# Norms summed between the weight tiles and handed on in blocks of four chunks, in a two-block transformer kernel

## The reference

```python
def rms_norm(x, g):                       # _rmsnorm of the second block is the same
    return x * lax.rsqrt(jnp.mean(x * x, axis=-1, keepdims=True) + 1e-6) * g

# first block: dilated attention and pooling, then 128*128 experts
xn = rms_norm(h, norm1_g) * (1 + scale1) + shift1        # norm a1
...
h = h + gate1 * (merged @ w_out)
xn2 = rms_norm(h, norm2_g) * (1 + scale2) + shift2       # norm b1
h = h + gate2 * peer_ffn(xn2, ...)                       # peer_wq, top-k, gelu(x @ down.T) * gates @ up
x = rms_norm(h, final_g)                                 # norm f1
# second block: joint attention with 256 context tokens, then a gated convolution FFN
hx = _rmsnorm(x, norm1_w) * (1 + s1) + sh1               # norm a2
hc = _rmsnorm(ctx, norm1_w) * (1 + s1c) + sh1c           # norm ctx
...
x = x + g1 * (heads @ w_o)
h2 = _rmsnorm(x, norm2_w) * (1 + s2) + sh2               # norm b2
x = x + g2 * (silu(conv3(h2 @ w_up_gate)) * (h2 @ w_up)) @ w_down
return _rmsnorm(x, final_w)                              # norm f2
```

## Time and profile before

| | |
|---|---|
| three runs | 4014.66, 4017.24, 4024.36 us; median 4017.24 us |
| the profiled execution | 4012.41 us, of which the span on the engines is 4010.6 us |
| TensorE matmul busy | 3630.9 us of the span |
| VectorE, ScalarE busy | 2671.8 us, 1656.7 us |
| mean granted TensorE clock | 0.961 of full speed |

### The profile page before, as it was taken

One profiled execution on the slowest core, in us unless ns is written; L12 is line 12 of the kernel. 1 busy time (PEld: TensorE's weight loads), 2 busy tenths in 40 slices (PEclk: granted clock), 3 DMA queues, 4 the chain that ended last, 5 costly groups with the idle time before them and its releaser, 6 DMA issues.

```text
span 4010.6 us, 73869 instructions
## 1 busy us (share of the span) xinstructions
PE 3630.9 (91%) x27694; PEld 3473.7 (87%) x27694; DVE 2671.8 (67%) x4416; ACT 1656.7 (41%) x2865; POOL 174.6 (4%) x240
## 2 busy tenths in 40 slices
PE   0899999883699999999999999889978989999998
PEld 0898888882599999999999999878945989999998
DVE  7875434589887878777777878652247566666554
ACT  0542112431254444444444544442226455555443
POOL 0000000002500000000000000000000000000000
PEclk8899999996899999999999999999999989999999
DMA  9887764441467676777767676522220435555554
GB/s 411 330 308 265 273 262 147 146 148 42 142 237 303 237 282 250 274 262 264 269 258 293 234 292 241 200 105 95 95 74 1 158 135 182 186 188 185 171 183 141
DMA packets 129659, 829.35 MB, mean 207 GB/s; under 512 B 12784, under 2 KB 29296, under 8 KB 38256
## 3 DMA queue, kind: packets, MB, share of 16 engines
q1 hardware_dynamic: 87984, 619.20, 42.2%
q0 software_dynamic: 24768, 189.80, 12.4%
q10 hardware_dynamic: 16640, 16.78, 1.2%
HBM read 806.86 MB, written 18.87 MB: 206 GB/s over the span
## 4 chain that ended last, share of the span: by engine, by line
PE 87%; DVE 8%; DMA 2%; issue 2%; ACT 1%; DVEq 0%; SPq 0%; POOL 0%; ACTq 0%; POOLq 0%
PE ps L874 23%; PE ps L872 23%; PE ps L873 23%; PE ps L847 8%; DMA arena<-in_ada 2%; PE ps L907 1%; PE ps L909 1%; PE ps L910 1%; PE ps L841 1%; DVE arena L1473 1%; DVE arena L1474 1%; PE ps L1152 0%; DVE x_low L1265 0%; ACT arena L506 0%; PE ps L861 0%
## 5 line engine op out<-in xcount | busy, mean ns | idle before, releaser
L506 ACT ACTIVATE w_parts<-ring 128x512 fp32r<-128x512 f32 x1352 | 841.4, 632 | 1078.8 <-PE ps L874 860.2
L874 PE MATMUL ps<-x_high,ring_low 128*128 128x256 f32 (+1 forms) x4448 | 1279.6, 288 | 0.0
L1251 DVE TENSOR_TENSOR ring_low<-ring,w_parts 128x512 fp32r<-128x512 f32 x1352 | 882.8, 689 | 526.3 <-ACT w_parts L506 504.9
L872 PE MATMUL ps<-x_high,w_parts 128*128 128x256 f32 (+1 forms) x3040 | 879.5, 289 | 110.4 <-DVE ring_low L1251 110.4
L873 PE MATMUL ps<-x_low,w_parts 128*128 128x256 f32 (+1 forms) x3040 | 878.0, 289 | 0.0
L874 PEld LDWEIGHTS ps<-x_high,ring_low 128*128 128x128 f32 x4448 | 858.7, 193 | 7.2
L872 PEld LDWEIGHTS ps<-x_high,w_parts 128*128 128x128 f32 x3040 | 575.2, 189 | 120.4 <-DVE ring_low L1251 96.3
L873 PEld LDWEIGHTS ps<-x_low,w_parts 128*128 128x128 f32 x3040 | 576.2, 190 | 8.4
L874 PE MATMUL ps<-at_high,ring_low 128*128 128x256 f32 x2048 | 577.5, 282 | 0.0
L872 PE MATMUL ps<-at_high,w_parts 128*128 128x256 f32 x2048 | 575.5, 281 | 0.0
L873 PE MATMUL ps<-at_low,w_parts 128*128 128x256 f32 x2048 | 575.5, 281 | 0.0
(11 more groups left out here) (210 smaller groups left out, 5288.3 us busy)
## 6 DMA issues: line engine op xcount, KB each, us to landing
ada<-in_ada POOLq DMA_DIRECT2D x160, 1024.0 KB, 6.9
ring<-in_peer_down SPq DMA_DIRECT2D x128, 1024.0 KB, 5.0
ring<-in_peer_up SPq DMA_DIRECT2D x128, 1024.0 KB, 5.3
ring<-in_w_in SPq DMA_DIRECT2D x102, 1024.0 KB, 5.4
ring<-in_w_up SPq DMA_DIRECT2D x88, 1024.0 KB, 4.8
ring<-in_w_down SPq DMA_DIRECT2D x64, 704.0 KB, 4.0
arena<-in_ada SPq DMA_DIRECT2D x32, 1024.0 KB, 19.3
ring<-in_w_out SPq DMA_DIRECT2D x16, 1024.0 KB, 4.8
```

What stands on the lines that cost most here:

```text
L506: return nc.scalar.activation(*a, **k)
L872: mm(to, w_high, high(k), start=(k == 0), stop=False)
L874: ins = mm(to, w_low, high(k), start=False, stop=(k == k_all - 1))
L1251: vv.tensor_tensor(ring_low[:, slot, cols], ring[:, slot, cols], parts[:, m, 0:w].bitcast(F32), ALU.subtract).then_inc(lo_ready, 1)
```

## The change

Five norms are rebuilt (b1, a2 with f1 merged into it, ctx, b2, f2); a1, kv and q stay.

1. The squares are made chunk by chunk in the stage before, behind the eviction of the chunk: in ScalarE's program the square of chunk n-3 stands behind the four copies of tile n (wo, wo2), and the squares of chunk u-19 behind the copies of tile u+1 (last expert turn; there two squares per chunk, of h and of h times final_g). In stage down they stand in blocks of four, and four single ones.
2. TensorE sums a chunk between tiles: chunk u-1 behind tile u (wo, wo2), chunk u-18 twice, into banks 4 and 5, behind tile u of the last expert turn, which is unrolled for it; in down 12 chunks behind the third tile of the last group and four behind the fourth.
3. f1 and a2 share one chain: the mean of a2's squares follows from the two sums. The final scaling of the first block (`to_next`) and the whole norm ctx go into the q2 stage of the second block.
4. The activations go over in four blocks of four chunks: VectorE multiplies a block by the reciprocal root (`unit`), ScalarE applies gain and shift to each chunk and copies the block's high part (`shift_high`), VectorE subtracts (`x_low`).
5. The first two tiles of the next stage (wq, q2, up) are split before the norm's end, in buffers that lie free, and `split_pair` runs piece j of both tiles as soon as block j is there.
6. The output is scaled and written in four DMAs. The small reductions of the last expert turn are spread otherwise over its tiles, and the context is loaded during it.

```diff
@@ ScalarE, stage wo (wo2 is the same with its names)
-            for n in range(16):
-                tile_in("wo", 0, 0, n)
-                high(WO, "wo", 0, 0, n, n % RING)
-            act.wait_ge(h_ready, 1)
-            norm("b1", hT, X, X, mod1[:, 48:64], high_to=XH)
+            for n in range(KC + 3):
+                if n < 16:
+                    tile_in("wo", 0, 0, n)
+                    high(WO, "wo", 0, 0, n, n % RING)
+                elif n < 18:
+                    tile_in("wq", 0, 0, n - 16)
+                    high(WP, "wq", 0, 0, n - 16, n - 16, fresh=True)
+                else:
+                    root_table()
+                if n >= 3:
+                    c = n - 3
+                    act.wait_ge(acc_free, BANKS + OUTS["wo"] + c + 1)
+                    square(sq1[:, c, :], hT[:, c, :])
+            root("b1")
+            shift_high("b1", sq1, X, XH, coef, mod1[:, 48:64])
@@ ScalarE, new helpers
+            def square(dst, src, **k):
+                act_fn(dst, src, ACT.Square, **k).then_inc(sq_ready, 1)
+            def root(name, **k):
+                act.wait_ge(mean_ready, RUN[name] + 1)
+                act_fn(rs[:, 0:T], rs[:, 0:T], ACT.Sqrt, **k).then_inc(root_ready, 1)
+            def root_table():
+                act_fn(small[:, 15:16], cst("ones")[:, 0:1], ACT.Sqrt)
+            def shift_high(name, z, x, xh, gain, shift, blocks=range(4)):
+                at = KC * RUN[name]
+                for b in blocks:
+                    act.wait_ge(unit_ready, at // 4 + b + 1)
+                    for k in range(4 * b, 4 * b + 4):
+                        act_fn(x[:, k, :], z[:, k, :], ACT.Identity, bias=shift[:, k:k + 1],
+                               scale=gain[:, k:k + 1]).then_inc(x_ready, 1)
+                    act.wait_ge(x_ready, at + 4 * b + 4)
+                    act_fn(xh[:, 4 * b:4 * b + 4, :], x[:, 4 * b:4 * b + 4, :], ACT.Copy).then_inc(xh_ready, 1)
@@ ScalarE, last expert turn, behind high() of tile u+1
+                    if last and u >= 19:
+                        squares_of(u - 19)
+                    if last and u in (30, 31):
+                        tile_in("in2", 0, 0, u - 30)
+                        act.wait_ge(a_free, TWO + 64 + 96)
+                        high(W2, "q2", 0, 0, u - 30, u - 30, fresh=True)
+            def squares_of(c):
+                act.wait_ge(acc_free, BANKS + OUTS["peer"] + 32 * (NG - 1) + 16 + c + 1)
+                square(sq_h[:, c, :], hT[:, c, :])
+                square(sq_g[:, c, :], hT[:, c, :], scale=vc("final_g")[:, c:c + 1])
@@ ScalarE, between the blocks
-            norm("f1", hT, X, None)
-            norm("ctx", ...)
-            norm("a2", ...)
+            root_table()
+            for c in (14, 15):
+                squares_of(c)
+            root("a2", scale=1.0 / D)
+            act_fn(rs[:, T:2 * T], rs[:, T:2 * T], ACT.Sqrt).then_inc(root_first, 1)
+            shift_high("a2", sq_h, X2[:, :, CTX:], X2H[:, :, CTX:], coef_f, mod2[:, 0:KC])
+            act.wait_ge(ctx_in, 16)
+            for b in range(4):
+                square(sq_ctx[:, 4 * b:4 * b + 4, :], ctxT[:, 4 * b:4 * b + 4, :])
@@ TensorE
+            def split_pair(name, i, per, parts, to, high, low, x_low):
+                for j in range(PIECES):
+                    pe.wait_ge(xl_ready, x_low + j + 1)
+                    for t in range(2):
+                        ins = piece(to[t], parts, PIECES * t + j, ...)
...
+            def sum_squares(name, c, ready, sqd, b=4, last=False):
+                pe.wait_ge(sq_ready, SQUARES[name] + ready)
+                ins = mm(ps[:, b, 0:T], ones, sqd[:, c, :], start=(c == 0), stop=(c == KC - 1))
+                if last:
+                    ins.then_inc(sum_ready, 1)
+            def split_summed(name, parts, high, low, run):
+                for u in range(16):
+                    bank(OUTS[name] + u)
+                    split_tile(name, 0, 0, u, ...)
+                    if u:
+                        sum_squares(run, u - 1, u, sq1)
+                sum_squares(run, KC - 1, KC, sq1, last=True)
+            def sum_both(c):
+                sum_squares("a2", c, 2 * c + 2, sq_h)
+                sum_squares("a2", c, 2 * c + 2, sq_g, b=5, last=(c == KC - 1))
-            with pe.Fori(0, NG) as i:
+            with pe.Fori(0, NG - 1) as i:
                 for u in range(32):
+                    expert_tile(i, u)
+            for u in range(32):
+                expert_tile(NG - 1, u)
+                if u >= 18:
+                    sum_both(u - 18)
+            for c in (14, 15):
+                sum_both(c)
+            split_pair("q2", 0, 0, W2, ...)
+            for c in range(KC):
+                sum_squares("ctx", c, c // 4 + 1, sq_ctx, last=(c == KC - 1))
+            for u in range(2, 8):
+                bank(OUTS["q2"] + u)
+                split_tile("q2", 0, 0, u, ps[:, u % BANKS, 0:T], W2, x_high, x_low)
+            pe.wait_ge(xl_ready, X_LOW["ctx"] + 4)
+                    if last and n == 2:               # stage down, last group
+                        for c in range(12):
+                            sum_squares("f2", c, c // 4 + 1, X)
+                    if last and n == 3:
+                        for c in range(12, KC):
+                            sum_squares("f2", c, c - 8, X, last=(c == KC - 1))
@@ VectorE
+            def split_unit(name, src, z, x, xh, xl):  # unit: one 128x1024 multiply; x_low: one 128x1024 subtract
+                unit(src, z, 0)
+                unit(src, z, 1)
+                x_low(name, x, xh, xl, 0)
+                unit(src, z, 2)
...
-            norm("b1", hT, X, coef)
-            shifted_lows("b1", X, XH, XL, mod1[:, 48:64])
+            mean("b1")
+            invert("b1")
+            split_unit("b1", hT, sq1, X, XH, XL)
+            for n in range(2, 30):                    # q2 and on: low() of tile n, and in between
+                low(W2, SPLIT["q2"] + PIECES * n + 1, n, n % RING)
+                if n == 2:
+                    mean("ctx")
+                if n == 3:
+                    invert("ctx")
+                    for b in range(4):
+                        unit(ctxT, ctxT, b)
+                if n in (5, 6):
+                    for b in range(2 * (n - 5), 2 * (n - 5) + 2):
+                        x_low("ctx", X2[:, :, 0:CTX], X2H[:, :, 0:CTX], X2L[:, :, 0:CTX], b)
...
+                if 10 <= n < 18:
+                    to_next(2 * n - 20)
+                    to_next(2 * n - 19)
@@ ScalarE, in the same stage: behind the copies of tile n+1
+                if n == 2:
+                    root("ctx")
+                if n in (4, 5):
+                    shift_high("ctx", ctxT, X2[:, :, 0:CTX], X2H[:, :, 0:CTX], coef, modc[:, 0:KC],
+                               range(2 * (n - 4), 2 * (n - 4) + 2))
@@ SyncE
-            sp.wait_ge(scaled, before("f2", "scaled") + KC)
-            sp.dma_start(out, hT[:]).then_inc(out_done, 16)
+            for b in range(4):
+                sp.wait_ge(final_ready, KC + 4 * (b + 1))
+                sp.dma_start(out[:, 4 * b:4 * b + 4, :], hT[:, 4 * b:4 * b + 4, :]).then_inc(out_done, 16)
```

More of the change, by code:

```diff
@@ L785, in _ @@
                     high(WO2, "wo2", 0, 0, 0, 0)
[L786 to L791, removed]
+            for n in range(1, KC + 3):
+                if n < 16:
+                    tile_in("wo2", 0, 0, n)
+                    high(WO2, "wo2", 0, 0, n, n % RING)
+                elif n < 18:
+                    tile_in("up", 0, U, n - 16)
+                    high(WF, "up", 0, U, n - 16, n - 16, fresh=True)
+                else:
+                    root_table()
+                if n >= 3:
+                    c = n - 3
+                    act.wait_ge(acc_free, BANKS + OUTS["wo2"] + c + 1)
+                    square(sq1[:, c, :], hT[:, c, :])
+            root("b2")
+            shift_high("b2", sq1, X, XH, coef, mod2[:, 48:64])
             def gate_row(i, p):
@@ L1022, in _ @@
             pe.wait_ge(keys_in, 16)
-            for n in range(16):
+            split_pair("wq", 0, 0, WP, [ps[:, (OUTS["wq"] + t) % BANKS, 0:T] for t in range(2)],
+                       lambda k: XH[:, k, :], lambda k: XL[:, k, :], X_LOW["b1"])
+            for n in range(2, 16):
                 o = OUTS["wq"] + n
@@ L1174, in _, with up_tiles @@
                     ins.then_inc(sub_sum, 1)
-            pe.wait_ge(xl_ready, 8 + 3 * KC + 4)
-            split_loop("wo2", WO2, MH, ML)
-            norm_sum("b2", X, KC)
-            pe.wait_ge(xl_ready, 12 + 4 * KC)
-            with pe.Fori(0, FF // 4) as i:
-                for u in range(U):
+            pe.wait_ge(xl_ready, X_LOW["ctx"] + 4 + 4)
+            split_summed("wo2", WO2, MH, ML, "b2")
+            split_pair("up", 0, 0, WF, [ps[:, (OUTS["up"] + t) % BANKS, 0:T] for t in range(2)],
+                       lambda k: XH[:, k, :], lambda k: XL[:, k, :], X_LOW["b2"])
+            def up_tiles(i, first):
+                for u in range(first, U):
```

(21 more changed lines are left out.)

211 lines of the change are left out of this document (128 added, 83 removed).

## The result

The changed kernel takes 4065.11 us (median of 4 runs, 4059.63 to 4068.26) against 4017.97 us for the kernel before on the same chip: 1.0109 times as long, 95% interval 1.0097 to 1.0121. I had forecast 4016 us, no measurable change, with 4000 to 4037 as the range. It is slower, and by more than my range allowed.

A forecast was written before the change was run, and what follows sets the result against it. TensorE's matmuls, 91% of the span, bound the kernel; 135 us of holes between stages were the target. Terms -6.5 - 5.8 + 7.8 + 4.2 + 1.6 = +1.3 us gained gave 4016 us, range 4000 to 4037.

The forecast's parts named there:

- b1: Stage wo and the turn behind it: hole shrinks by 15.5 us, stalls and sums cost 22.0, net 6.5 us slower.
- the blocks: Last expert turn and the turn between blocks: 39.9 us gained, 32.1 paid back in stalls and sums, net 7.8 us faster.
- b2: Stage wo2 and the turn behind it: 16.2 us gained, 22.0 given back in stalls and sums, net 5.8 us slower.
- f2: Last norm and output at the end: 15.1 us against 24.75, less 5.4 for 12 sums, net 4.2 us faster.
- the unrolled turn: Last expert turn written out on TensorE: one loop-jump wait at a turn's border goes, 1.6 us faster (bounds 0 and 1.7).
- the quarter of the output: Last output DMA, 512 KB, at the kernel's end: 3.7 us from a line through measured DMAs, 3.2 by the skill.
- A: Rival, faster: the squares come in time for TensorE, so 52 us would stay, 3964 us; chance 0.08.
- B: Rival, slower: granted clock falls in the new stalls; 4036 us if 12 between the blocks fell, 4081 if all 38; chance 0.14.
- C: Rival, slower: ctx's parts come late beside q2's tiles; 17 us, 4033 if none covered, partly 4020 to 4030; chance 0.12.
- ctx's 16 sums: TensorE's sums for the ctx norm, following the pair of first tiles between the blocks: a cost of 7.2 us.

The follow-up runs named there:

- e1: The kernel before with only an unused tile of 64 bytes per partition put behind coef, moving the arena up: 4066.08 us, ratio 1.0116.
- e2: The changed kernel with coef_f laid into modt, so every other tile lies where it lay in the kernel before: 4017.58 us, ratio 1.000.
- e11: The kernel before with only TensorE's loop of expert turns run seven times and the eighth turn written out: 4016.14 us, ratio 0.9995.
- e4: The kernel before with an unused tile of 88 bytes per partition ahead of the arena, which then starts at a multiple of 512: 4017.93 us, ratio 1.0002.
- e3: The changed kernel with ScalarE's squares of 13, 13 and 12 chunks ahead of the tile's four copies instead of behind them: 4007.38 us, ratio 0.9973.
- e5: The changed kernel with the edits of e2 and e3 together, old arena place and squares ahead of the copies: 3963.61 us, ratio 0.986.
- e6: The kernel before with the weights' high parts of stages qk, v, wq and the experts alone 64 bytes higher: 3967.71 us, one run.
- e7: The kernel before with the 64-byte tile of e1 and the weight buffers W1 and WP another 64 bytes higher: 4035.1 us, one run.
- e8: The kernel before with an unused tile of 24 bytes, so the arena starts at 64 modulo 128: 4025.87 us, one run.
- e10: The kernel before with 48 bytes more ahead of the arena, which then starts at 88 modulo 128: 4058.23 us, one run.
- e9: The changed kernel with the edits of e2, e3 and e6 together: 3923.64 us, ratio 0.9761, 3908.01 to 3933.28 in 5 runs.

## Why the prediction was wrong

**The step that failed.** It is the one that is not in the sum: in the terms of b1, of the blocks, of b2 and of f2 I costed instructions, waits and DMAs, and never the new tile. Every other stage was taken to go on as before, with "757 matmuls, 0.118 us each". The allocation moved the activations of 24,480 matmuls by 64 bytes, and the weights of two in three of them, and they lost 2.1 ns each on average. With this one term, as e1 measured it, put right the forecast is 4016 + 48 = 4064 us, against 4065.11. The Trainium skill ("SBUF — State Buffer", Specifications) gives SBUF cachelines of 16 bytes; by that alone 64 bytes would change nothing, and starts at 40 and 104 modulo 128 lie alike in such lines. The measured 48 us decide: for these matmuls the two starts are not alike.

**The steps that held.** e2 is the change without the shift, so its trace tests the sum. Its marks are the first matmuls of wo, wq, q2, wo2 and up:

```profile
667.29 0.55 PE L959 MATMUL ps<-merged_high,w_parts_out 128*128 128x256 f32 x1 [7.21 <-DVE ring_low L1428]
...
793.70 0.55 PE L959 MATMUL ps<-x_high,w_parts 128*128 128x256 f32 x1 [8.59 <-issue]
...
2629.29 0.58 PE L959 MATMUL ps<-x_high,w_parts 128*128 128x256 f32 x1 [9.00 <-DVE x_low L1396]
...
3119.95 0.39 PE L959 MATMUL ps<-heads_high,w_parts_out 128*128 128x256 f32 x1 [1.86 <-DVE heads_low L1804]
...
3245.35 0.58 PE L959 MATMUL ps<-x_high,w_parts_ff 128*128 128x256 f32 x1 [8.54 <-DVE x_low L1396]
```

| stretch, us | before | e2 | after | e2 less before | forecast |
|---|---|---|---|---|---|
| start to wo | 667.1 | 667.3 | 670.4 | +0.2 | 0 |
| wo to wq | 117.3 | 126.4 | 127.9 | +9.1 | +6.5 |
| wq to wo2 | 2330.2 | 2326.3 | 2356.4 | -3.9 | -9.4 |
| wo2 to up | 119.5 | 125.4 | 126.6 | +5.9 | +5.8 |
| up to the end | 776.5 | 771.8 | 784.9 | -4.7 | -4.2 |
| span | 4010.6 | 4017.1 | 4066.3 | +6.5 | -1.3 |

The last column repeats the terms of b1, of the blocks with the unrolled turn (-7.8 - 1.6), of b2 and of f2. From the last split matmul's end to the next stage's first, e2 and the changed kernel have holes of 10.3 us at b1 and b2 (forecast 9.8), 11.6 between the blocks (11.6), and 14.0 to the end (15.1). Together the holes shrink by 88.6 us, and the prediction's own terms add up to 88.5; its remark that the change takes 40 us out of them counts only what lies between the blocks. In e2's stage wo a stalled tile comes every 763.57 - 756.18 = 7.39 us, 1.74 over the old 5.65 where I had 1.66; in the last expert turn every 8.22 us, 2.57 over where I had 2.6. At the end the 14.0 us are fewer than 15.1 because the quarter of the output lands in 2.6 us (median of four) and not 3.7; the 3.2 that the prediction takes from the Trainium skill's fit, which is given for DMAs issued by GpSimd, is too long for this one of SyncE as well.

The +9.1 at b1 against +6.5, and the +5.9 at b2 that agrees, hold some luck. Stage wo's first tile, part of it at the lower clock, took 8.25 us in e2 and 7.03 before; wo2's first tile took 7.29 in e2 and 8.49 before. These 1.2 us, once more and once less, belong to the stages' starts and not to stalls or sums; without them both stretches lie 1.3 to 1.4 us above the forecast.

**The unrolled turn.** Its 1.6 us held: without the jump the last border has no wait, and the turn ahead of it takes 181.0 us in e2 and in e11, against 182.6. The 5.5 us between -3.9 and -9.4 come from the other turns: five of them are 5 x 1.2 = 6 us longer in e2's trace than in that of the kernel before. e4 has them as long with the loop of eight, so the unrolling isn't needed for it; how much of it is scatter between executions isn't shown, as the kernel before has only one trace. The spans of the two profiled executions differ by 6.5 us, and the medians of the runs (4017.58 and 4017.97) don't. Why the granted clock falls behind some borders and not behind others stays open.

**The rivals.** A (squares in time) didn't happen. Its price of 52 us was about right, though: e3 brings it about by moving the squares and gains 58 us, e5 against e2 54, and e5 ends at 3963.6, where A had 3964. B (the clock falls in the stalls) didn't happen: the squares' stalls leave it at full. TensorE in e2's stages wo and wo2 and in the last expert turn, with the granted clock behind the count:

```profile
676.00:783.00 107.00, 93.68 (x745) 1.00 0.43 148
2514.00:2612.00 98.00, 82.34 (x630) 1.00 0.56 202
3128.00:3234.00 106.00, 92.68 (x736) 1.00 0.44 149
```

C (ctx late) didn't: between q2 and wo2 e2 takes 490.7 us against 3114.58 - 2630.00 = 484.6, +6.1, which is less than the 7.2 that I had for ctx's 16 sums; the one wait of TensorE for a low part there is 0.32 us.

**Open.** What decides the pitch for given places of the operands, and what decides at a border which of two pitches e6's placement takes, the runs don't tell. They show the dependence at five starts of the arena, and of the two operands apart for one group of stages; e6, e7, e8 and e10 have one run each, with its trace.

## What to carry to other kernels

Where an engine is busy 91% of the time with one instruction, read its pitch in a stretch that the edit doesn't touch, before and after: matmuls per 100 us at full clock took one view and found what no wait shows. Cost an allocation like an instruction; place a new small tile behind the large buffers or in a dead one, and try a few starts of the matmul operands on purpose: here one cost 48 us, and another gained 40 (e9 against e5) to 52 (e6). Before a difference of a few us between two traces is put down to an edit, look at a second trace without the edit: e4's turns are as long as e11's. And a helper's work in an in-order queue belongs ahead of the instruction that waits for the end of the bound engine's piece: with it behind, the rebuilt norms gained nothing, and moving it ahead gained 58 us.

## What the runs showed of the hardware

- The pitch of back-to-back float32r matmuls of 128x128 by 128x256, each with its own weight load, at full clock depends on where their operands start: 0.1178 us with activations and two of three weights at 0 or 40 modulo 128 bytes, 0.1183 at 64, 0.1200 at 88 and 104, and 0.1133 with these weights at 104 and the activations at 40. The third weight lay at 0 throughout, and its matmul took on the pitch of the others. With 512 columns the shift from 40 to 104 went the other way, from 0.2311 to 0.2268 us. The Trainium skill ("TensorE: Matmul & The Clock Gate", Wait — 56ns, not 53.3ns?) gives columns over 2.4 GHz and about 2.5 ns; worked out for 256 columns that is an estimate of 0.1092 us, which no placement here reached.
- In the placement of 104 and 40 there are two pitches, 0.1133 and 0.1178 us. In e6 each of turns 2 to 7, about 180 us long, has one of them throughout; in e9 it also changed within stage qk.
- A stall of 1.02 or 1.42 us behind every tile leaves the granted clock at 1.00 in the three stages that have them. Behind single waits of 1.9 to 3.3 us it fell in some places (to 0.57 over 4 us behind 1.93 us in e4, to 0.56 behind 2.61 in e2) and in others not (1.00 behind 3.27 in e2).
